# A hybrid decoder trunk on one core: operands, weights, modulation units and normalisation of layer 0 take other places in the engines' orders

## What is computed

```python
def reference(x, c, ...):
    c_act = jax.nn.silu(c)
    for layer in range(DEPTH):
        mod = c_act @ mod_w[layer] + mod_b[layer]
        shift, scale, gate = jnp.split(mod, 3, axis=-1)
        h = rmsnorm(x, norm_g[layer]) * (1.0 + scale[:, None, :]) + shift[:, None, :]
        if layer % 2 == 0:
            y = even_mixer(h, ...)
        else:
            y = odd_mixer(h, ...)
        x = x + gate[:, None, :] * y
    return rmsnorm(x, final_g)

def even_mixer(h, w_in, ...):
    xa, ga, gb_post, gc_pre, v, gb = jnp.split(h @ w_in, EVEN_SPLITS, axis=-1)
    ya = rg_lru(causal_dwconv(xa, conv_w, conv_b), w_a, b_a, w_x, b_x, lam)
    yb = gb_post * causal_dwconv(gc_pre * v, sc_conv_w)
    y = jnp.concatenate([ya * jax.nn.silu(ga), yb * jax.nn.silu(gb)], axis=-1)
    return y @ w_out
```

## Time and profile before

| | |
|---|---|
| median of three runs | 1356.64 us |
| the profiled execution | 1361.12 us, span 1359.3 us |
| TensorE busy | 1302.8 us, 96% |
| VectorE, ScalarE, GpSimd busy | 951.6, 632.5, 318.7 us |
| chain that ended last | PE 80%, DVE 11%, ACT 4%, issue 3%, DMA 1% |
| DMA | 174.15 MB, mean 128 GB/s |

### The profile page before, as it was taken

The page is one execution under the profiler, slowest core; times in us unless marked ns, Lnnn a source line. Parts: engine busy times, 40 slices in busy tenths (PEclk is TensorE's granted clock), DMA queues, the critical chain, the costliest instruction groups (busy, mean ns, idle before and its releaser), DMA issues.

```text
span 1359.3 us, 15668 instructions
## 1 busy us (share of the span) xinstructions
PE 1302.8 (96%) x5735; PEld 1071.8 (79%) x5735; DVE 951.6 (70%) x1118; ACT 632.5 (47%) x880; POOL 318.7 (23%) x190
## 2 busy tenths in 40 slices
PE   4998999999999999899999989998999999999997
PEld 4877788878887888688878868887887888888886
DVE  6888887878877796695667787747758647334554
ACT  6456456554646465333365554143143243223654
POOL 0024444534433332030300232132132130000000
PEclk7898999999999999999899989998999999999998
DMA  9911342323233242496738202320320321853463
GB/s 310 300 47 36 93 128 56 104 82 108 66 109 93 82 128 68 153 379 215 232 129 257 84 4 63 107 77 32 109 78 32 109 78 62 309 188 113 164 220 121
DMA packets 152864, 174.15 MB, mean 128 GB/s; under 512 B 7180, under 2 KB 115924, under 8 KB 152788
## 3 DMA queue, kind: packets, MB, share of 16 engines
q1 hardware_dynamic: 152788, 173.15, 39.6%
HBM read 143.76 MB, written 29.36 MB: 127 GB/s over the span
## 4 chain that ended last, share of the span: by engine, by line
PE 80%; DVE 11%; ACT 4%; issue 3%; DMA 1%; SPq 0%; ACTq 0%; DVEq 0%
PE psum L2062 26%; PE psum L2063 26%; PE psum L2064 26%; DVE X L1455 1%; DVE win L1925 1%; DVE w_lo L1365 1%; PE psum L2188 1%; PE psum L2380 1%; ACT w_hi L858 1%; DMA whole_x<-in_x 1%; ACT whole_x L1182 0%; DVE X L1461 0%; DVE w_lo L1388 0%; DMA raw<-in_hy_w_out 0%; DVE d_lo L1935 0%
## 5 line engine op out<-in xcount | busy, mean ns | idle before, releaser
L2062 PE MATMUL psum<-X,w_hi 128*128 128x512 f32 x1396 | 551.3, 395 | 21.9 <-DVE w_lo L1380 15.8
L2063 PE MATMUL psum<-X,w_hi 128*128 128x512 f32 x1396 | 547.1, 392 | 0.0
L2064 PE MATMUL psum<-X,w_lo 128*128 128x512 f32 x1396 | 546.8, 392 | 0.0
L2062 PEld LDWEIGHTS psum<-X,w_hi 128*128 128x128 f32 x1396 | 264.5, 189 | 84.6 <-issue 28.4
L2064 PEld LDWEIGHTS psum<-X,w_lo 128*128 128x128 f32 x1396 | 264.3, 189 | 55.6
L2063 PEld LDWEIGHTS psum<-X,w_hi 128*128 128x128 f32 x1396 | 264.5, 189 | 54.6 <-issue 0.5
L1365 DVE TENSOR_TENSOR w_lo<-raw,w_hi 128x1024 fp32r<-128x1024 f32 (+2 forms) x98 | 103.7, 1060 | 144.0 <-ACT w_hi L858 143.8
L858 ACT ACTIVATE w_hi<-raw 128x1024 fp32r<-128x1024 f32 (+2 forms) x98 | 89.6, 915 | 187.8 <-PE psum L2064 163.1
L881 ACT ACTIVATE w_hi<-ssum 128x512 fp32r<-128x512 f32 x140 | 86.8, 625 | 112.8 <-PE psum L2064 86.8
L1388 DVE TENSOR_TENSOR w_lo<-ssum,w_hi 128x512 fp32r<-128x512 f32 x140 | 115.9, 834 | 29.0 <-ACT w_hi L881 28.4
L810 POOL TENSOR_TENSOR ssum<-ssum,raw 128x512 f32<-128x512 f32 x35 | 54.7, 1562 | 305.3 <-DVE w_lo L1388 305.3
(11 more groups left out here) (240 smaller groups left out, 1858.4 us busy)
## 6 DMA issues: line engine op xcount, KB each, us to landing
raw<-in_hy_w_in SPq DMA_DIRECT2D x48, 512.0 KB, 5.1
raw<-in_pool_w_in SPq DMA_DIRECT2D x32, 512.0 KB, 5.2
bufs<-y_dram SPq DMA_DIRECT2D x48, 256.0 KB, 4.1
whole_x<-y_dram SPq DMA_DIRECT2D x48, 256.0 KB, 3.4
aux<-in_mod_w SPq DMA_DIRECT2D x16, 512.0 KB, 3.9
y_dram<-bufs SPq DMA_DIRECT2D x16, 512.0 KB, 2.7
raw<-in_hy_w_out SPq DMA_DIRECT2D x16, 512.0 KB, 5.6
raw<-in_mod_w SPq DMA_DIRECT2D x16, 512.0 KB, 5.1
```

What stands on the lines that cost most here:

```text
L2062: nc.tensor.matmul(out_, whi, xhi, start=first, stop=False, skip_group_check=check)
L2063: nc.tensor.matmul(out_, whi, xlo, start=False, stop=False, skip_group_check=check)
L2064: return nc.tensor.matmul(out_, wlo, xhi, start=False, stop=last, skip_group_check=check)
```

## The change

Head 0 and head 1: on VectorE `low_t(0, 0)` goes ahead of `softplus`, `low_t(0, 1)` ahead of the short taps, the second half of `t2_and_t4`, `lo(0, 0)`, `lo(0, 2)` and the other `low_t` ahead of `m_squared`; `reset` and `inputs_of_scan` of head 0 go behind `lo(0, 3)`; `low_t4` goes behind later operands in two halves. ScalarE makes `hi(0, 0)`, `hi(0, 2)`, `hi(0, 3)` and the tanh earlier. In every head `take_22` of pair C goes from the next head's beginning to a place ahead of `reset`. `window_counts` goes from head 3 to step 12 of pass C. The splits of W and y of the first steps of pass A go into head 7, and a third step is split ahead of the loop. The sixteen units are loaded and added in steps 3 to 15 instead of 0 to 15, two each in steps 5, 8 and 11. In pass B the row sums follow step 4 (before, 5), the root comes with step 7 (8), the broadcast follows step 6 (8), and the blocks are normalised one in each of the steps 9 to 14 and two in step 15 (before, two in each of the steps 11 to 14), the modulation on ScalarE one step later than the normalisation.

No instruction but a table load is added or removed, and TensorE's order differs only in the places of the row sums and the broadcast.

```diff
@@
+NORMAL_AT = {**{25 + k: (k,) for k in range(6)}, 31: (6, 7)}
+MODS_AT = ((), (), (), (0,), (1,), (2, 3), (4,), (5,), (6, 7), (8,), (9,), (10, 11), (12,), (13,), (14,), (15,))
@@ LOADS
             if layer == 0 and p == "A":
-                LOADS.append(mods1[n])
+                LOADS.extend(mods1[m] for m in MODS_AT[n])
@@ SyncE, pass A
-                    ring_load(mods1[at])
-                    if at == 2:
+                    for m in MODS_AT[at]:
+                        ring_load(mods1[m])
+                    if at == 3:
                         spill_head(HEADS - 1, 0)
-                    if at == 3:
                         spill_head(HEADS - 1, 1)
@@ ScalarE, head 0
             gate_i(0)
+            hi(0, 0)
+            decay_tanh(0)
             upper_t(0, 2)
-            decay_tanh(0)
             decays(0)
             decay_squares(0)
+            hi(0, 2)
             upper_t(0, 3)
+            hi(0, 3)
             root_of_head(0)
-            first_operands(0)
@@ ScalarE, heads
                 prep(cc, 5)
+                if i == HEADS - 1:
+                    split_hi(("W", 0, "A", TIME_ORDER[0]))
+                    act.wait_ge(a_ready, HEADS)
+                    split_y((0, "A", TIME_ORDER[0]))
+                    act.wait_ge(aux_done, 2 * KB)
+                    split_y((0, "A", TIME_ORDER[1]))
                 root_of_head(i)
                 prep(cc, 6)
-            split_hi(("W", 0, "A", TIME_ORDER[0]))
-            act.wait_ge(a_ready, HEADS)
-            split_y((0, "A", TIME_ORDER[0]))
-            act.wait_ge(aux_done, 2 * KB)
-            split_y((0, "A", TIME_ORDER[1]))
+            split_hi(("W", 0, "A", TIME_ORDER[1]))
             take_21(Q["C", HEADS - 1])
-            split_hi(("W", 0, "A", TIME_ORDER[1]))
             sigmoid_b(HEADS - 1)
+            split_hi(("W", 0, "A", TIME_ORDER[2]))
             act.wait_ge(sgb_done, HEADS)
+            split_y((0, "A", TIME_ORDER[2]))
@@ ScalarE, passes
-                    if (p, at) == ("B", 8):
+                    if (p, at) == ("B", 7):
                         root(layer, 0)
-                    if p == "B" and 11 <= at < 15 and layer == 0:
-                        for k in (2 * at - 22, 2 * at - 21):
+                    if layer == 0:
+                        for k in NORMAL_AT.get(n - 1, ()):
                             modulate(0, k)
-                        for k in (2 * at - 22, 2 * at - 21):
                             round_h(0, k)
@@ VectorE, heads
-                if i > 1:
-                    take_22(cc - 3)
                 prep(a, 0)
+                if i == 1:
+                    reset(0)
+                    inputs_of_scan(0)
                 recur(i - 1)
@@
-                if i == 3:
-                    window_counts()
                 prep(cc, 5)
                 m_squared(i)
+                if i == HEADS - 1:
+                    first = [s for s in STEPS if s[0] == 0][:3]
+                    step_splits(first[0])
+                    split_y(first[1])
                 add_12(cc)
                 prep(cc, 6)
                 gated_sc(i)
+                take_22(cc)
                 reset(i)
                 inputs_of_scan(i)
-            first = [s for s in STEPS if s[0] == 0][:2]
-            step_splits(first[0])
-            split_y(first[1])
-            take_22(Q["C", HEADS - 1])
             recur(HEADS - 1)
             split_lo(("W",) + first[1])
+            gate_b(HEADS - 1)
             out_a(HEADS - 1)
-            gate_b(HEADS - 1)
+            step_splits(first[2])
             out_b(HEADS - 1)
@@ TensorE, pass B
-                    if n == 5:
+                    if n == 4:
                         sum_rows(layer, 0)
-                    if n == 8 and layer == 0:
+                    if n == 6 and layer == 0:
                         broadcast(0)
```

More of the change, by code:

```diff
@@ L1216, in passes @@
                         squares(layer, 1, range(at - 5, at - 4))
-            passes(0, 2)
+            passes(0, 3)
             split_hi(("V0", 0))
@@ L1687, in _ @@
             t2_and_t4(0, 1)
+            low_t(0, 0)
             softplus()
+            low_t(0, 1)
             for n in range(2):
@@ L1712, in _ @@
                 out_a(i - 1)
-                if i == 1:
-                    for kp in range(KP):
-                        low_t4(0, kp)
                 prep(a, 2)
@@ L1718, in _ @@
                 prep(a, 3)
+                if i == 1:
+                    for kp in (0, 1):
+                        low_t4(0, kp)
                 gate_b(i - 1)
                 prep(a, 4)
+                if i == 1:
+                    for kp in (2, 3):
+                        low_t4(0, kp)
                 out_b(i - 1)
```

36 lines of the change are left out of this document (17 added, 19 removed).

## The result

Four executions of the changed kernel took 1337.73 to 1339.92 us, median **1338.41**; four of the kernel before 1354.77 to 1356.75, median 1356.62. The ratio is 0.987, with a 95% interval of 0.9856 to 0.9883: 18.2 us, with an uncertainty of about 2. Four more executions on another chip had a median of 1339.96 against 1356.7, ratio 0.987 (0.9857 to 0.9884). The change is faster, by the amount forecast and a little more (1340.5, range 1334.5 to 1347).

What follows compares the result with a forecast made beforehand. TensorE, busy 1302.8 of 1359.3 us, was taken as the bound, so only its waits and clock count. Gains of 4.3 + 2.8 + 7.4 + 1.6 = 16.1 us took the median from 1356.64 to 1340.5 us, range 1334.5 to 1347.

Steps and rivals of the forecast that it cites:

- A: End of head 0: VectorE, its two pauses filled, reaches `take_22` 4.9 us earlier; gain 4.3 us, bounds 2.5 to 9.2.
- the charge of 1.1 - 0.5 for one more meeting with GpSimd: Earlier T sums on GpSimd hold up one more VectorE operation: 1.1 us, less 0.5 for the chance of none.
- The waits that were to reappear: In head 1, TensorE waits about 4 us in all, at `lo(1, 0)` and product 4.
- B: Head boundaries in layer 0: `take_22` earlier and divisor steps moved shorten waits of 1.14 and 1.62 us; gain 2.8 us.
- the sentence on the other boundaries: At head boundaries other than the two counted, VectorE may wait for product 7 by a few tenths; cost nothing.
- C: Start of pass A of the output projection: of 8.1 us lost, 0.7 remains; gain 7.4 us, at least 4.
- The two slacks: Start of pass A: operands ready ahead of TensorE by 0.8 us at step 2 and 1.3 us at step 4.
- D: End of pass B: one block a step, modulated a step behind VectorE, removes a 1.64 us wait; gain 1.6 us.
- The first (TensorE-bound, 21 in all): End of head 0: VectorE isn't the bound, gain there up to 9.2 us, total 21, time 1335.6; chance 0.12.
- The second (given back): Steps 2 and 4 of pass A miss, head 1 stalls or `take_22` stays late: total 10, about 1346.5; chance 0.22.
- The third (the ring of four slots): Pass A: loads wait for modulation additions, steps about 9 us instead of 5.44, 36 us over 10 steps, 1376; chance 0.03.
- The fourth (the waits only move on): All four places: waits go but reappear at the next operand, time within 0.2% (2.7 us); chance 0.03.

Runs made afterwards that it cites:

- units early: Changed kernel with modulation units fetched one per step from step 0 of pass A again, the early splits kept: 1344.83 us, ratio 0.9911.
- heads 0/1: Changed kernel with heads 0 and 1 of layer 0 back in the old order on ScalarE and VectorE: 1342.9 us, ratio 0.9898.
- boundaries: Changed kernel with `take_22` back at the next head's start and the divisors' steps back in head 3: 1342.77 us, ratio 0.9887.
- take_22: Changed kernel with only `take_22` back at the next head's start, the divisors' steps staying in pass C: 1341.29 us, ratio 0.9883.
- pass A: Changed kernel with the start of pass A back in the old order, both splits and modulation units: 1345.15 us, ratio 0.9907.
- softplus: Changed kernel with 16 small VectorE steps, 3.3 us in sum, added ahead of softplus: 1340.06 us, ratio 0.9877.
- both of the last two: Changed kernel with head 1's urgent VectorE work first and block 5 last in step 0 of pass A, 1334.06 us; same with `add_gate(0)` earlier, 1334.97 us.

## Why the prediction came out right, step by step

**The bound.** TensorE's waits and its clock were the whole of it: all four places answered at TensorE, and none of the busy time that fell on other engines had to be counted.

**A, 4.3 forecast, 5.4 and 5.5 measured.** The step that decided, "VectorE sets when product 4 starts, so 4.9 and not 9.2", is shown in three ways: the undone order costs 5.5, a cost added to VectorE arrives in full (3.2), a cost taken from it comes back in full (3.4). After, VectorE stands idle for 0.9 us in all between 89 and 137:

```profile
89.00:137.20 48.20, 45.12 (x196) 36.21 (x196) 47.26 (x64) 30.55 (x42) 19.07 (x11) 1.00 0.22 69
```

The term that failed is the charge of 1.1 - 0.5 for one more meeting with GpSimd. The early sums did fall on softplus and the taps, as said, but as many operations were drawn out before as after, and they lost 0.4 us less in all. That and the two pauses, 4.9, make up the 5.4. The waits that were to reappear are there, 0.81 at `lo(1, 0)` and 2.15 at product 4, 3.0 in sum where about 4 was said. `gate_a(0)` had no slack: the wait of 3.12 us once softplus took 3.2 longer shows it.

**B, 2.8 forecast, 4.5 between the two kernels (the table's 4.0, and 0.5 that it counts at step 0), 4.5 undone.** The mechanism was right, the size was that of the two waits in the list. What failed is the sentence on the other boundaries, where I feared a loss of some tenths; they had one of 0.2 to 0.4 us each before, and it went. Splitting the edit shows that at head 4 it needed both parts.

**C, 7.4 forecast, 7.3 by the leads (18.16 - 10.87), of which 1.3 is clock; 6.1 undone.** From step 0 to 3 it took 556.53 - 536.51 = 20.0 us, as said, with the one wait of 0.69. The two slacks were 1.1 for step 2 (its y is split by 549.97, needed at 551.09; forecast 0.8) and 2.7 for step 4 (559.30 against 561.97; forecast 1.3). The load for step 4 was issued at 551.51 and landed 4.85 us later where I had taken 5.83 from the earlier trace rows. Why both halves are needed was not in the prediction. On the table of the sigmoid: its load and the sigmoid behind it stand at

```profile
543.49 1.28 ACT L1061 ACT_TABLE_LOAD   x1
544.78 1.06 ACT L1061 ACTIVATE bufs<-bufs 128x1024 f32<-128x1024 f32 x1
```

so 1.28 us, with the sigmoid 0.01 us behind its end. The Trainium skill's "ScalarE: Activation LUTs", section "What ACT_TABLE_LOAD costs", gives 2.66 us for a switch with its drain; this trace shows no drain on either side of the load. The trace decided rightly.

**D, 1.6 forecast, 2.6 measured, by the leads and undone.** A second wait of 0.39 in the step before (0.40 when undone) was left out of the sum. The row sums and the broadcast cost nothing that shows.

**The sum.** 16.1 forecast, 19.7 by the leads, of which C holds 1.3 of clock, and 18.7 by the four places undone. The times give 18.2 and 16.7 on two chips. A, B and D came out too small; C was right only together with its clock. I took nothing off for the clock of the profiled execution of before, which stood 4.5 above its median with a mean of 0.975: the executions nearer the median had 0.98 to 0.983, so the traced one had more of lower clock to lose than most. The two errors point in opposite directions, so it is in part luck that the forecast of the end missed by only 2 us. The mechanism at each place doesn't rest on that.

**The rivals.** The first (TensorE-bound, 21 in all) is out by the undone order. The second (given back) is out for B and C. But at the end a milder form of it can't be excluded: every edit that costs moved the end less than its place (units early: less than 6.5), by 0.1 to 2.3 us, every one that gains gained more, by 1.5 to 4, and the ends of the four parts undone add up to 12.0 of 17.6 us. In seven of these profiles (heads 0/1, boundaries, take_22, pass A, softplus, both of the last two) the lower clock at the column sums lasts 3.4 or 6.8 us in place of 10.2. All these ends are taken from one reference, whose ratio is itself uncertain by 1.8 us and whose two profiles have the longest such stretch, so the shift may be its own; this is not settled. The third (the ring of four slots) did not occur: no wait in pass A has a load behind it. The fourth (the waits only move on) is out by the leads, which last to the end.

## What to carry to other kernels

Where an operand is made ready early, look for the engine that will set the next start, and take its idle time, not the waiting engine's, as the gain; here that was 4.9, and 5.4 came, of 9.2. When an operation is moved on one engine, read the DMA queue for what waits for it there: by the rows, the spill of a result moved back by 14 us held a load that had nothing to do with it. An edit with two halves in one pass is to be priced as a whole, since the wait at the next step can take most of what one half gains alone.
